# Hybrid decoder layer on one core: the late modulation rows summed as an f32r high part and an f32r rest, with output rows between

## What is computed

```python
mod = jax.nn.silu(c) @ w_ada[l] + b_ada[l]                    # 6 rows of 1024
sh1, sc1, g1, sh2, sc2, g2 = jnp.split(mod, 6, axis=-1)
h = rmsnorm(x, pre_mix_gain[l]) * (1.0 + sc1) + sh1
y = token_mixer(h, w_in[l], ..., w_out[l], rel_bias, lambda_init)   # attention heads, then y @ w_out
x = x + g1 * rmsnorm(y, post_mix_gain[l])
h = rmsnorm(x, pre_ffn_gain[l]) * (1.0 + sc2) + sh2
y = hier_moe(h, w_group[l], ..., w_gate[l], w_up[l], w_down[l])     # 32 SwiGLU experts
x = x + g2 * rmsnorm(y, post_ffn_gain[l])
```

## Time and profile before

| | us |
|---|---|
| median of 3 runs (lowest, highest) | 740.93 (740.45, 741.03) |
| the profiled execution's own time | 740.76 |
| its span, first to last instruction | 739.0 |
| PE busy in the span | 712.1 (96%) |
| DVE busy | 643.0 (87%) |
| ACT busy | 524.5 (71%) |
| POOL busy | 147.1 (20%) |

### The profile page before, as it was taken

How to read it: one execution, slowest core, us unless ns; L and a number is a source line. 1 busy time by engine, 2 the same in 40 slices (tenths; PEclk the granted TensorE clock), 3 DMA queues, 4 the chain that set the end, 5 groups by cost and what they waited for, 6 DMA issues and landing times.

```text
span 739.0 us, 13136 instructions
## 1 busy us (share of the span) xinstructions
PE 712.1 (96%) x4857; PEld 567.5 (77%) x4859; DVE 643.0 (87%) x573; ACT 524.5 (71%) x573; POOL 147.1 (20%) x190
## 2 busy tenths in 40 slices
PE   6999999998899999999999999999999999999994
PEld 6785775446678888888888888888888888888873
DVE  3734869467789999999999999999999999999995
ACT  4011433546478888888888888888888888888882
POOL 5600110310311221111111221111111221111000
PEclk9999999997999999999999999999999999999998
DMA  9999996926498999999999999999999999999901
GB/s 321 350 368 404 409 378 262 393 90 228 156 338 304 375 382 383 372 376 381 376 377 380 379 380 378 381 366 387 375 381 377 382 375 383 381 374 375 350 1 60
DMA packets 102153, 249.20 MB, mean 337 GB/s; under 512 B 5265, under 2 KB 5325, under 8 KB 100077
## 3 DMA queue, kind: packets, MB, share of 16 engines
q1 hardware_dynamic: 99648, 244.33, 88.7%
q0 software_dynamic: 1008, 3.31, 1.2%
q10 hardware_dynamic: 1470, 1.22, 0.5%
HBM read 247.78 MB, written 1.07 MB: 337 GB/s over the span
## 4 chain that ended last, share of the span: by engine, by line
PE 88%; DVE 7%; ACT 2%; DMA 1%; issue 1%; SPq 0%; DVEq 0%; ACTq 0%
PE PS L1491 49%; PE PS L1479 8%; PE PS L1440 6%; PE PS L1197 4%; PE PS L1458 4%; PE PS L1449 4%; PE PS L1358 4%; PE PS L1241 3%; DVE MOD L786 2%; PE PS L1235 2%; DMA W<-in_w_ada_dram 1%; PE PS L1125 1%; DVE S L865 1%; PE PS L1150 1%; PE PS L1469 1%
## 5 line engine op out<-in xcount | busy, mean ns | idle before, releaser
L1037 DVE TENSOR_TENSOR WL<-W,WH 128x2048 fp32r<-128x2048 f32 x185 | 417.4, 2296 | 9.8 <-ACT WH L690 9.8
L690 ACT CAST WH<-W 128x2048 fp32r<-128x2048 f32 x185 | 346.6, 1907 | 0.0
L1491 PE MATMUL PS<-WH,XT 128*128 128x512 f32 x512 | 142.5, 400 | 1.4 <-DVE XT L1056 1.4
L1491 PE MATMUL PS<-WL,XT 128*128 128x512 f32 x508 | 138.2, 393 | 0.0
L1491 PEld LDWEIGHTS PS<-WL,XT 128*128 128x128 f32 x508 | 95.3, 188 | 22.4
L1491 PEld LDWEIGHTS PS<-WH,XT 128*128 128x128 f32 x512 | 93.7, 188 | 21.3 <-DVE XT L1056 1.5
L457 POOL COPY cur<-PG 128x2 f32 (+1 forms) x31 | 5.7, 184 | 371.2 <-PE PS L1469 370.9
L1491 PE MATMUL PS<-WH,HT 128*128 128x512 f32 x248 | 70.4, 406 | 1.6 <-DVE HT L1068 1.6
L1491 PE MATMUL PS<-WL,HT 128*128 128x512 f32 x248 | 68.6, 398 | 0.0
L469 POOL CAST cur<-PG 128x6 bf16 (+1 forms) x31 | 58.5, 1887 | 0.0
L1491 PEld LDWEIGHTS PS<-WH,HT 128*128 128x128 f32 x248 | 44.9, 190 | 16.6 <-issue 8.0
(11 more groups left out here) (228 smaller groups left out, 881.5 us busy)
## 6 DMA issues: line engine op xcount, KB each, us to landing
W<-in_w_gate_dram SPq DMA_DIRECT2D x64, 1024.0 KB, 8.2
W<-in_w_down_dram SPq DMA_DIRECT2D x64, 1024.0 KB, 6.4
W<-in_w_up_dram SPq DMA_DIRECT2D x63, 1024.0 KB, 9.4
W<-in_w_ada_dram SPq DMA_DIRECT2D x16, 1024.0 KB, 7.9
W<-in_w_in_dram SPq DMA_DIRECT2D x12, 1024.0 KB, 7.7
W<-in_w_ada_dram SPq DMA_DIRECT2D x16, 512.0 KB, 5.3
W<-in_w_out_dram SPq DMA_DIRECT2D x4, 1024.0 KB, 7.3
toe<-line_dram POOLq DMA_DIRECT2D x1, 1536.0 KB, 11.7
```

What stands on the lines that cost most here:

```text
L690: nc.scalar.copy(WH[(UPE * odd + u) % SPLITS][:], source).then_inc(hi_ready, 1)
L1037: nc.vector.tensor_tensor(low, source, WH[(UPE * odd + u) % SPLITS][:].bitcast(f32), ALU.subtract).then_inc(lo_ready, 1)
L1491: last = nc.tensor.matmul(PS[:, bank, :], lhsT, w[:, q * 512:(q + 1) * 512], start=begin, stop=end)
```

## The change

The sum over the partitions is made with f32r matmuls. ScalarE rounds the tile of part a to f32r (`mod_high`), VectorE subtracts that from the tile, which leaves the exact rest, also f32r (`mod_low`), and TensorE multiplies both with a matrix of ones in f32r, two matmuls for each bank, adding in PSUM. High and rest, `rowHL`, lie where `hT` was (8 KB a partition); there is one of them, so `mod_high(a+1)` waits for the matmuls of part a. GpSimd makes the ones (`onesR`) at the start. The order on the three engines is changed with it. The memory plan moves: a spacer of 768 columns takes the place of what was over of the first third of `gain`, which now has two rows.

```diff
+        early.enter_context(nc.sbuf_tensor("spacer", [P, D - 2 * P], f32))
+        gain = sb("gain", [P, 2, D], at=early)
+        before = sb("before", [P, P], at=early)[:]
+        onesR = sb("onesR", [P, P], f32r, at=early)
         qkT = sb("qkT", [P, 16, SEQ], at=early)
-        hT = sb("hT", [P, DC, SEQ], at=early)
+        with nc.sbuf_tensor("hT", [P, DC, SEQ], f32) as h:
+            hT = h
+        rowHL = sb("rowHL", [P, 2, D], f32r, at=early)
...
+            nc.gpsimd.tensor_copy(onesR[:], ones[:]).then_inc(ones_in, 1)
             nc.gpsimd.memset(S[:, 0, 0, 0:2 * P], 0.0).then_inc(bank_zero, 1)
             nc.gpsimd.memset(MOD[:, 2 * D:], 0.0).then_inc(rest_zero, 1)
...
+            def mod_high(part):
+
+                act.wait_ge(ada_used, DC * (part // 2))
+                if part == 2:
+                    act.wait_ge(win_used, 12)
+                else:
+                    act.wait_ge(mod_mm, part - 2)
+                nc.scalar.copy(rowH, MOD[:, part * D:(part + 1) * D]).then_inc(sum_high, 1)
+
+            mod_high(2)
             transposed(5)
             outputs(4)
             exps(7)
+            transposed(6)
+            mod_high(3)
             mod_row_copy(2)
-            transposed(6)
             outputs(5)
+            transposed(7)
+            mod_high(4)
             mod_row_copy(3)
-            transposed(7)
             outputs(6)
             act.wait_ge(sq_mm, 1)
             nc.scalar.activation(st[:, 56:64], PS[:, 7, 0:N_DIFF * TT], ACT.Sqrt, bias=epsb[:],
                                  scale=1.0 / (2 * HEAD)).then_inc(rms_ready, 1)
+            mod_high(5)
             mod_row_copy(4)
             outputs(7)
             mod_row_copy(5)
...
+            def mod_low(part):
+
+                dve.wait_ge(sum_high, part - 1)
+                nc.vector.tensor_tensor(rowL, MOD[:, part * D:(part + 1) * D], rowH.bitcast(f32), ALU.subtract).then_inc(sum_low, 1)
+
             for g in range(PAIRS):
                 scores(g)
                 ada(4 + g + max(g - 4, 0))
                 if 4 <= g < PAIRS - 1:
                     ada(5 + g + (g - 4))
+                if g == PAIRS - 1:
+                    mod_low(2)
                 probabilities(g)
             ada(15)
+            mod_low(3)
+            mod_low(4)
 
             dve.wait_ge(rms_ready, 1)
             nc.vector.reciprocal(st[:, 56:64], st[:, 56:64]).then_inc(inv_rms, 1)
+            mod_low(5)
...
             def sum_part(a):
 
-                pe.wait_ge(ada_used, DC * (a // 2))
+                pe.wait_ge(sum_low, a - 1)
                 if a == 2:
+                    pe.wait_ge(ones_in, 1)
                     pe.wait_ge(proj_ready, 12)
                 else:
                     pe.wait_ge(mod_row, a - 2)
-                sum_rows(mod_parts(a), 0)
+                for b in range(2):
+                    for part in (rowH, rowL):
+                        last = nc.tensor.matmul(PS[:, b, :], onesR[:], part[:, 512 * b:512 * b + 512], start=(part is rowH), stop=(part is rowL))
+                last.then_inc(mod_mm, 1)
...
             weigh_values(4)
-            sum_part(2)
-            weigh_values(5)
-            transpose_probabilities(6)
             pe.wait_ge(score_read, 2 * PAIRS)
             values_out(4)
             project_out(1, [4], True, False)
-            sum_part(3)
+            weigh_values(5)
+            transpose_probabilities(6)
+            sum_part(2)
             weigh_values(6)
             transpose_probabilities(7)
             values_out(5)
             project_out(1, [5], False, False)
-            sum_part(4)
+            sum_part(3)
             weigh_values(7)
             values_out(6)
             project_out(1, [6], False, False)
-            sum_part(5)
+            sum_part(4)
             spread_inverse(0)
             values_out(7)
             project_out(1, [7], False, False)
+            sum_part(5)
             spread_inverse(1)
```

More of the change, by code:

```diff
@@ L152, in build @@
         line = sb("line", [N_BIAS, 3 * P], at=early)
-        gain = sb("gain", [P, 3, D], at=early)
-        before = gain[:, 0, 0:P]
+        early.enter_context(nc.sbuf_tensor("spacer", [P, D - 2 * P], f32))
+        gain = sb("gain", [P, 2, D], at=early)
+        before = sb("before", [P, P], at=early)[:]
+        onesR = sb("onesR", [P, P], f32r, at=early)
         qkT = sb("qkT", [P, 16, SEQ], at=early)
-        hT = sb("hT", [P, DC, SEQ], at=early)
+        with nc.sbuf_tensor("hT", [P, DC, SEQ], f32) as h:
+            hT = h
+        rowHL = sb("rowHL", [P, 2, D], f32r, at=early)
         MOD = sb("MOD", [P, 6 * D], at=early)
@@ L162, in build @@
         sq = MOD[:, 0:D]
+        rowH, rowL = rowHL[:, 0, :], rowHL[:, 1, :]
         diag = MOD[:, D:2 * D].rearrange("p (n q) -> p n q", n=N_DIFF * TT)
@@ L211, in build @@
         gate_turned = sem("gate_turned")
+        sum_high, sum_low, ones_in = sem("sum_high"), sem("sum_low"), sem("ones_in")
         first_onehot, gates_ready, pg_filled = (sem(n) for n in ("first_onehot", "gates_ready", "pg_filled"))
@@ L421, in _ @@
             with nc.allow_non_contiguous_dma(reason="router columns"):
-                pool.dma_start(gain[:, 1, :], on_all(post_mix_gain, D)).then_inc(gain_in, 16)
-                pool.dma_start(gain[:, 2, :], on_all(pre_ffn_gain, D)).then_inc(gain_in, 16)
+                pool.dma_start(gain[:, 0, :], on_all(post_mix_gain, D)).then_inc(gain_in, 16)
+                pool.dma_start(gain[:, 1, :], on_all(pre_ffn_gain, D)).then_inc(gain_in, 16)
                 pool.dma_start(G2[:], on_all(post_ffn_gain, D)).then_inc(gain_in, 16)
@@ L448, in _ @@
             pool.wait_ge(mod_row, 1)
-            nc.gpsimd.tensor_tensor(MOD[:, 2 * D:3 * D], MOD[:, 2 * D:3 * D], gain[:, 1, :], ALU.mult).then_inc(gained, 1)
+            nc.gpsimd.tensor_tensor(MOD[:, 2 * D:3 * D], MOD[:, 2 * D:3 * D], gain[:, 0, :], ALU.mult).then_inc(gained, 1)
             pool.wait_ge(mod_row, 3)
-            nc.gpsimd.tensor_tensor(MOD[:, 4 * D:5 * D], MOD[:, 4 * D:5 * D], gain[:, 2, :], ALU.mult).then_inc(gained, 1)
+            nc.gpsimd.tensor_tensor(MOD[:, 4 * D:5 * D], MOD[:, 4 * D:5 * D], gain[:, 1, :], ALU.mult).then_inc(gained, 1)
             pool.wait_ge(mod_row, 4)
```

## The result

| | before | changed |
|---|---|---|
| median of the runs, us | 740.98 (740.45 to 742.56, 4 runs) | 748.27 (745.55 to 752.54, 4 runs) |
| ratio of the changed to the one before | | 1.0106, 95% interval 1.0083 to 1.0129 |
| profiled execution, us | 740.76 | 748.25 |
| its span, us | 739.0 | 746.5 |

The change makes the kernel slower by 1.1%; 747.2 us were forecast. In a later series the same kernel gave 749.48 (746.19 to 749.93, 5 runs), ratio 1.0120 (1.0099 to 1.0141).

The account below looks back on a forecast made before the run. TensorE bounds the kernel, through when `project_out(0, ...)` starts: waits of 11.4 us against 3.12 + 1.23 + about 0.5 saved put it 6.4 later. 739.0 + 6.4 + 1.76 = 747.2 us, range 744.0 to 751.0.

Parts of the forecast that it names:

- The hand-over from TensorE to ScalarE: Timetable price: 0.27 us from TensorE's last matmul of a sum to ScalarE's start.
- The seams: Gaps between matmul groups on TensorE: 0.3 us credited of some 0.5; about 0.5 with starts in the total.
- its third wait: TensorE idle ahead of `weigh_values(6)`, behind ScalarE's cast, row copy and `outputs(5)`: 0.27 + 0.95 + 0.90 + 0.37 + 0.14 = 2.65 us.
- its timetable: Last stage, `project_out(0, ...)`, starts at 155.7 in place of 149.3, 6.4 us later, with waits of 11.4 us.
- after the first wait the loss would be taken up by the wait for `mod_low(2)`: A clock fall behind the first wait, ahead of `sum_part(2)`, would be absorbed; only falls behind later waits cost up to 1.7.
- the loop's 1.7 us: One clock fall behind a 1.56 us wait in the loop: 40 matmuls take 11.04 in place of 9.33 us.
- one fall gives 749.0: Rival: the clock falls in the new waits, up to 1.7 us each behind second and third; two give 750.7; chance 0.24.
- A later stage spared: Rival: the clock fall between the logit groups comes later, returning 1.65 there and about 0.9 in transposes; 744.7; chance 0.12.
- The other side: Rival: ScalarE is no bound, so the last stage starts 3.12 + 1.23 us earlier; 736.4; chance 0.04.
- What hid the rest: VectorE's four early subtractions end at about 168.8; about 2 of its 3.57 us wait for following work are left.

Follow-up runs that it names:

- a_outputs_first: Changed kernel with only ScalarE's order altered: each `outputs` ahead of `mod_high` and the row copy; 745.83 us, ratio to before 1.0064.
- e_sqrt_early: a_outputs_first with the square root moved directly behind the last exponentials and its reciprocal ahead of VectorE's last weight unit; 743.09 us, ratio to before 1.0019.
- b_f32_new_order: Changed kernel's order on TensorE and ScalarE, but f32 sums and no `mod_high` or `mod_low`; 747.83 us, ratio to before 1.0086.
- c_fill_wait: Changed kernel with eight 128-column identity matmuls in the first wait, behind `weigh_values(4)`; 750.30 us, ratio to before 1.0109.
- f_sum_in_wait: Changed kernel with the three engines' orders set anew: `outputs` first, square root early, `sum_part(2)` back in the first wait; 741.81 us, ratio to before 1.0009.
- i: f_sum_in_wait with five identity matmuls between `weigh_values(4)` and `weigh_values(5)`; 741.07 us, ratio to before 1.0003.
- h_sqrt_early_fill: e_sqrt_early with nine identity matmuls in its one long wait; 742.13 us, ratio to before 1.0020.
- g_f32_sum_in_wait: f_sum_in_wait with the f32 sums of before, no high and rest; 743.57 us, ratio to before 1.0024.

## Why the prediction was right

**The mechanism** was the one forecast, in the same places. Expected and measured idle of TensorE:

| ahead of | forecast | measured |
|---|---|---|
| `project_out(1, [4])`, by VectorE | 2.72 | 2.68 |
| `sum_part(2)`, by `mod_low(2)` | 0.99 | none |
| `weigh_values(6)`, by `outputs(5)` | 2.65 | 2.47 |
| `weigh_values(7)`, by `outputs(6)` | 2.64 | 2.47 |
| `project_out(1, [7])`, by `outputs(7)` | 1.78 | 1.34 |
| `project_out(0, ...)`, by the row copy | 0.56 | 0.24 |

That ScalarE's order causes the third, fourth and fifth is shown by a_outputs_first and e_sqrt_early, where they go but for 0.33; the last, 0.24, stays in every order and is the hand-over by way of the row copy. That the split is not the cause is shown by b_f32_new_order.

**The sizes.** `mod_high` holds the queue for 0.96, as taken (its row shows 1.05, but on ScalarE's timeline the row copy behind it starts at 138.75, 0.96 later); `mod_low` takes 1.22, as taken; four f32r matmuls 0.94, as taken. The hand-over from TensorE to ScalarE was priced at 0.27 and is about 0.1 in the chain (136.77 + 0.94 to 137.79): the 0.27 took 1.72 for the sum ahead of that copy, whose own row has 1.96, which leaves 0.03. It makes the waits 0.2 too long each. The seams were credited with 0.5 us of saving and cost 0.4 more in place of it. Two sums of the prediction are slightly off: the terms of its third wait make 2.63, not 2.65, and its waits less what is taken away make 6.6, where its timetable has 6.4.

**The step that failed**, though the time came out near, is "after the first wait the loss would be taken up by the wait for `mod_low(2)`". The low clock cost 2.67 us (130.76 to 136.77 in place of 3.34 us of work), and that wait could take up only the 0.99 that it had; the remaining 1.7 lay on the path. It was priced as if a fall cost the loop's 1.7 us in all. With it and the seams, less what the waits were shorter, the last stage starts at 157.15 in place of 155.7. The case counted as a rival at 0.24 chance ("one fall gives 749.0") is what the profiled execution shows, though behind the first wait and not the second. The low clock stands around that first wait in the profiles of the changed kernel (both), a, b and e, so with such a wait it should have been the forecast and not a rival; but in one of the two profiles of the changed kernel it fell ahead of the wait, so the wait alone does not explain it.

**Two rivals appear in part.** A later stage spared: the second logit group at 1.98 in b_f32_new_order and c_fill_wait, not in the changed kernel. In the changed kernel the loop's fall was absent instead, which gave 1.2 back; the stage itself was 1.4 worse than forecast and the routing 0.7. The total came within 1.1 us by errors of opposite sign, which is luck as far as the last microsecond goes; that the kernel would be slower by several us, and where, was not. The other side, TensorE's saved time deciding, is refuted for this order; e, f and i, with other orders, come back to the time of before and not under it.

What hid the rest held: VectorE's four early subtractions ended at 170.4 (161.54 + 8.90), and VectorE then waited 1.98 us for its next work at 172.4; about 2 had been forecast.

## What to carry to other kernels

An engine's program is a queue: before a step is put into it, look at what stands behind it and who waits for that. Here two copies that nobody needed yet were put ahead of a 0.4 us copy that TensorE needed at once, three times over, and that cost more than the faster matmuls gave. Work taken from the bound engine counts only if what replaces it does not end in a wait of that engine, and a wait on TensorE costs its own length and, where the clock falls around it, up to 2.7 us more here.

## What was not expected of the hardware

**GpSimd and VectorE slow each other.** In the changed kernel VectorE's subtraction of two SBUF tiles takes 1.23 us alone and 2.16 beside GpSimd products of two SBUF tiles, and the second of those 3.33 in place of 2.35. VectorE's timeline, then GpSimd's:

```profile
145.67 1.23 DVE L918 TENSOR_TENSOR rowHL<-MOD,rowHL 128x1024 fp32r<-128x1024 f32 x1 [5.57 <-ACT rowHL L630]
...
151.85 2.16 DVE L918 TENSOR_TENSOR rowHL<-MOD,rowHL 128x1024 fp32r<-128x1024 f32 x1 [3.21 <-ACT rowHL L630]
```

```profile
150.58 2.35 POOL L456 TENSOR_TENSOR MOD<-MOD,gain 128x1024 f32<-128x1024 f32 x1
152.91 3.33 POOL L458 TENSOR_TENSOR MOD<-MOD,gain 128x1024 f32<-128x1024 f32 x1
```

In e_sqrt_early `diag` meets the last weight unit (2.30 us, two SBUF inputs, no longer than elsewhere) on VectorE and takes 3.89 in place of 1.90:

```profile
137.42 3.89 POOL L449 TENSOR_TENSOR MOD<-ident,st 128x1024 f32<-128x1024 f32 x1 [40.46 <-DVE st L929]
```

The Trainium skill says so ("GPSIMD Engine Reference", section "8. Key points"): GpSimd shares its SBUF interfaces with VectorE, with contention where VectorE has two SBUF inputs. The rows agree, and give the size. They fit one waiting until the other has ended: of such a pair the instruction that began first keeps its usual time, and the other ends its own usual time behind it. The product from 150.58 keeps its 2.35 and ends at 152.93, the subtraction ends at 154.01, 1.1 us behind; the next product ends at 156.24, 2.2 behind that; `diag` in e_sqrt_early ends at 141.31, 1.8 behind the end of the weight unit at 139.55. The longest was `diag` in h_sqrt_early_fill, 5.03 us, behind a weight unit and a subtraction. In the changed kernel it cost nothing, since what waited for either came later: `mod_low(5)` ended at 154.0, its sum began at 154.6. In h_sqrt_early_fill it made the wait of 1.23 us ahead of `sum_part(4)`.

**A fall of the clock needs no long wait, and in two executions none at all.** In g_f32_sum_in_wait the clock fell inside a wait of 1.33 us, behind eight matmuls of one column and one `weigh_values`. In f_sum_in_wait it fell at 126.8 and in the second profile of the changed kernel at 126.75, with TensorE busy since before 112: those eight matmuls (1.95 us) and the start of `weigh_values(4)` stood ahead of it, the wait began only 1.1 to 1.5 us later. f_sum_in_wait by stretches (the last column but two is the granted clock):

```profile
125.00:126.50 1.50, 1.50 (x15) 1.50 (x14) 1.40 (x2) 1.50 (x4) 0.00 (x0) 1.00 0.98 380
126.50:127.90 1.40, 1.40 (x10) 0.75 (x9) 1.40 (x1) 0.12 (x1) 0.00 (x0) 0.63 1.02 410
```

The same matmuls ran with no fall in the kernel before, and the second and third waits of 2.47 us, between full matmuls, brought none in the changed kernel, while two falls came at or behind them in c_fill_wait. What decides was not found. The Trainium skill ("TensorE: Matmul & The Clock Gate", section "HAM oscillation — how this bites in real kernels") tells of short bursts between waits that start cold each time; the runs show it in part, at some of the waits and not in every execution, and the two falls with TensorE busy are not of that kind.

The nine timed executions of the changed kernel lie between 745.55 and 752.54. That the clock makes this spread was not shown: the stages' lengths in the profiles differ by stretches at the low clock, but the mean granted clock of a run does not order the nine (0.985 at 745.55, 0.977 at 748.25, 0.982 at 752.54).
